# Expert items of 32 tokens in four column groups of TensorE, gate-up pieces of 256 whole rows

## The reference: what is computed

```python
logits = h @ w_router + b_router                 # 256 x 32
top_val, top_idx = lax.top_k(logits, 4)
weights = softmax(top_val)
for each expert e, for the tokens xb that chose it:
    gu = xb @ w_gate_up[e] + b_gate_up[e]        # 1024 -> 2048
    gate = minimum(gu[:, :1024], 7)
    up = clip(gu[:, 1024:], -7, 7)
    act = (up + 1) * gate * sigmoid(1.702 * gate)
    y = act @ w_down[e] + b_down[e]              # 1024 -> 1024
    out[token] += weight * y
```

```
42 53 27 40 37 42 25 48 33 27 25 21 24 29 35 26
32 23 25 33 37 35 29 26 34 24 19 22 33 43 27 48
```

## Time and profile before

| | us |
|---|---|
| median of 3 runs (1546.7 to 1549.62) | 1549.33 |
| the profiled execution's span | 1549.3 |
| TensorE busy | 97% |
| VectorE busy | 30% |
| ScalarE busy | 19% |

### The profile page before, as it was taken

The page is one execution under the profiler, slowest core; times in us unless marked ns, Lnnn a source line. Parts: engine busy times, 40 slices in busy tenths (PEclk is TensorE's granted clock), DMA queues, the critical chain, the costliest instruction groups (busy, mean ns, idle before and its releaser), DMA issues.

```text
span 1549.3 us, 21348 instructions
## 1 busy us (share of the span) xinstructions
PE 1502.3 (97%) x8793; PEld 775.7 (50%) x8794; DVE 472.4 (30%) x845; ACT 293.0 (19%) x457; POOL 36.9 (2%) x87
## 2 busy tenths in 40 slices
PE   6999899999999999999999999999999999999997
PEld 3875786633333333333333333333333686699643
DVE  2577442412121121211211112111111233466844
ACT  2224312211111111111111111111111233112100
POOL 6000210000000000000000000000000000000000
PEclk9999998999999999999999999999999999999999
DMA  9956104999999999999999999999999933244430
GB/s 373 314 213 243 56 3 195 405 397 429 426 429 428 428 429 429 428 429 429 429 428 429 429 428 430 428 428 429 428 427 428 363 109 109 109 164 164 175 151 27
DMA packets 71972, 503.32 MB, mean 325 GB/s; under 512 B 5278, under 2 KB 8496, under 8 KB 46320
## 3 DMA queue, kind: packets, MB, share of 16 engines
q1 hardware_dynamic: 71026, 500.25, 78.6%
q10 hardware_dynamic: 894, 2.30, 0.4%
HBM read 501.49 MB, written 1.05 MB: 324 GB/s over the span
## 4 chain that ended last, share of the span: by engine, by line
PE 81%; DMA 15%; DVE 2%; ACT 1%; issue 0%; SPq 0%; DVEq 0%
PE psum L1157 21%; DMA ring<-in_w_gate_up 13%; PE psum L1196 12%; PE psum L1458 6%; PE psum L1429 6%; PE psum L685 5%; PE psum L1114 3%; PE psum L1247 3%; PE psum L1098 3%; PE psum L614 3%; PE psum L1189 2%; PE psum L1032 2%; PE psum L1382 2%; DMA ring<-in_w_ada 2%; PE psum L1150 1%; PE psum L732 1%
## 5 line engine op out<-in xcount | busy, mean ns | idle before, releaser
L1157 PE MATMUL psum<-ring,work 128*64 128x512 f32 x2048 | 448.7, 594 | 11.3 <-DMA ring<-in_w_gate_up 11.3
L1157 PEld LDWEIGHTS psum<-ring,work 128*64 128x64 f32 x2048 | 142.6, 137 | 315.2 <-issue 289.2
L1196 PE MATMUL psum<-ring,work 128*64 128x512 f32 x1024 | 226.8, 595 | 0.0
L2235 DVE TENSOR_SCALAR work<-psum 128x512 f32<-128x512 f32 x32 | 22.1, 692 | 451.8 <-PE psum L1157 451.8
L1196 PEld LDWEIGHTS psum<-ring,work 128*64 128x64 f32 x1024 | 70.7, 137 | 153.9 <-issue 153.9
L1730 ACT ACTIVATE work<-work 128x512 f32<-128x512 f32 x32 | 20.1, 629 | 399.4 <-DVE work L2235 399.4
L685 PE MATMUL psum<-ring 128*128 128x256 f32 (+1 forms) x368 | 80.5, 380 | 0.4 <-ACT ring L1534 0.4
L685 PEld LDWEIGHTS psum<-ring 128*128 128x128 f32 (+1 forms) x368 | 68.5, 187 | 13.1 <-issue 2.1
L1114 PE MATMUL psum<-work 64*128 64x256 f32 x528 | 65.9, 389 | 0.7 <-ACT work L1736 0.7
L1736 ACT ACTIVATE work<-psum 128x512 f32<-128x512 f32 x32 | 19.1, 597 | 241.2 <-PE psum L1196 241.2
L1114 PEld LDWEIGHTS psum<-work 64*128 64x128 f32 x528 | 48.3, 186 | 31.9 <-issue 26.0
(11 more groups left out here) (476 smaller groups left out, 1533.9 us busy)
## 6 DMA issues: line engine op xcount, KB each, us to landing
ring<-in_w_gate_up SPq DMA_DIRECT2D x128, 2048.0 KB, 30.9
ring<-in_w_down SPq DMA_DIRECT2D x72, 2048.0 KB, 28.1
ring<-in_w_ada SPq DMA_DIRECT2D x12, 2048.0 KB, 12.4
ring<-in_w_up SPq DMA_DIRECT2D x8, 2048.0 KB, 7.8
ring<-in_w_in SPq DMA_DIRECT2D x6, 2048.0 KB, 7.9
ring<-in_w_out SPq DMA_DIRECT2D x4, 2048.0 KB, 7.9
ring<-in_w_in_sb SPq DMA_DIRECT2D x4, 2048.0 KB, 20.2
ring<-in_w_mem_kv SPq DMA_DIRECT2D x1, 2048.0 KB, 9.1
```

The costliest lines, as they stand in the source:

```text
L1157: ins = mm(B(1 + u)[CAP * h:CAP * (h + 1), :], xe[:, k % 4, k // 4, :], w[:, k % 2, c0:c0 + 512], start=False, stop=k == KT - 1)
L1196: last = mm(B(3)[CAP * h:CAP * (h + 1), :], act[:, k % 4, k // 4, :], w[:, k % 4, 512 * h:512 * (h + 1)], start=False, stop=k == KT - 1)
```

## The change

`CAP` becomes 32. An item is at most 32 tokens, so an expert with 33 to 64 tokens takes two passes, and `N_ITEM` grows from 48 to 64. With 32 columns in the stationary operand, four matmuls stand side by side, in four column groups (`GROUPS`). A group q computes 256 output columns (`GW`): in gate-up 256 of gate and 256 of up in one matmul of 512 columns, in down 256. The results of gate and up share one bank, 128 rows by 256 each.

```diff
-CAP = 64
+CAP = 32
+GROUPS = P // CAP
+GW = D // GROUPS
...
             def moe_src(e, j):
                 if j < 4:
-                    h, c0 = j // 2, 2 * (j % 2)
-                    return a["w_gate_up"][0, e, 512 * h:512 * (h + 1), :].rearrange(
-                        "(p c) n -> p c n", c=4)[:, c0:c0 + 2, :]
+                    return a["w_gate_up"][0, e, GW * j:GW * (j + 1), :].rearrange("(p c) n -> p c n", c=2)
...
             def freed(j, g):
                 if j < 4:
-                    sp_.wait_ge(S("e_gu"), g * 5 + [1, 2, 3, 5][j])
+                    sp_.wait_ge(S("e_gu"), g * 4 + (j + 1))
...
                 for ti in range(TT):
-                    for h in range(2):
-                        last = mm(B(0)[CAP * h:CAP * (h + 1), :], sel[:, ti, :],
-                                  tok[:, ti, 512 * h:512 * (h + 1)], start=ti == 0, stop=ti == TT - 1)
+                    for q in range(GROUPS):
+                        last = mm(B(0)[CAP * q:CAP * (q + 1), 0:GW], sel[:, ti, :],
+                                  tok[:, ti, GW * q:GW * (q + 1)], start=ti == 0, stop=ti == TT - 1)
...
             def scatter():
-                for c in range(4):
-                    for h in range(2):
-                        m = 4 * h + c
-                        last = mm(bank2(4 + m // 2)[:, m % 2, :], ye[CAP * h:CAP * (h + 1), c * P:(c + 1) * P],
-                                  selT[CAP * h:CAP * (h + 1), :], start=False, stop=False,
+                for j in range(2):
+                    for q in range(GROUPS):
+                        last = mm(bank2(4 + q)[:, j, :], ye[CAP * q:CAP * (q + 1), j * P:(j + 1) * P],
+                                  selT[CAP * q:CAP * (q + 1), :], start=False, stop=False,
                                   skip_group_check=True)
...
-                    for u in range(2):
-                        for h in range(2):
-                            r0 = E_N * (2 * u + h)
-                            mm(B(1 + u)[CAP * h:CAP * (h + 1), :], one_e[r0:r0 + E_N, :], bgu[r0:r0 + E_N, :],
-                               start=True, stop=False)
...
+                    for j in range(4):
+                        landed(j)
+                        w = ring[:, slots[j], :].rearrange("p (c u q n) -> p c q u n", c=2, u=2, q=GROUPS)
+                        for c in range(2):
+                            for q in range(GROUPS):
+                                last = mm(B(1)[CAP * q:CAP * (q + 1), :], xe[:, c, j, :], w[:, c, q, :, :],
+                                          start=j == 0 and c == 0, stop=j == 3 and c == 1)
                         last.then_inc(S("e_gu"), 1)
+                        if j == 0:
+                            for q in range(GROUPS):
+                                mm(B(1)[CAP * q:CAP * (q + 1), :], one_e[E_N * q:E_N * (q + 1), :],
+                                   bgu[E_N * q:E_N * (q + 1), :], start=False, stop=False)
...
                     for c in range(4):
-                        last = tr(B(3)[:, c * P:(c + 1) * P], act_tm[:, c * P:(c + 1) * P])
+                        for b in range(2):
+                            last = mm(B(2)[HD * b:HD * (b + 1), c * HD:(c + 1) * HD], act_tm[:, c * HD:(c + 1) * HD],
+                                      ident[:, :].rearrange("p (h b s) -> p b h s", h=2, b=2)[:, b, :, :],
+                                      start=True, stop=True)
```

More of the change, by code:

```diff
@@ L1146, in expert @@
                     pe.wait_ge(S("e_selT"), g + 1)
-                    for u in range(2):
-                        for h in range(2):
-                            r0 = E_N * (2 * u + h)
-                            mm(B(1 + u)[CAP * h:CAP * (h + 1), :], one_e[r0:r0 + E_N, :], bgu[r0:r0 + E_N, :],
-                               start=True, stop=False)
[L1153 to L1165, removed]
-                        last.then_inc(S("e_gu"), 1)
[L1167 to L1171, removed]
+                    for j in range(4):
+                        landed(j)
+                        w = ring[:, slots[j], :].rearrange("p (c u q n) -> p c q u n", c=2, u=2, q=GROUPS)
+                        for c in range(2):
+                            for q in range(GROUPS):
+                                last = mm(B(1)[CAP * q:CAP * (q + 1), :], xe[:, c, j, :], w[:, c, q, :, :],
+                                          start=j == 0 and c == 0, stop=j == 3 and c == 1)
+                        last.then_inc(S("e_gu"), 1)
+                        if j == 0:
+                            for q in range(GROUPS):
+                                mm(B(1)[CAP * q:CAP * (q + 1), :], one_e[E_N * q:E_N * (q + 1), :],
+                                   bgu[E_N * q:E_N * (q + 1), :], start=False, stop=False)
                     gather(g + 2)
@@ L1185, in expert @@
                     turn_x(g + 2)
+                    for q in range(GROUPS):
+                        mm(B(3)[CAP * q:CAP * (q + 1), 0:GW], one_e[E_N * q:E_N * (q + 1), :],
+                           b_down[E_N * q:E_N * (q + 1), :], start=True, stop=False)
                     pe.wait_ge(S("e_actT"), g + 1)
-                    for h in range(2):
-                        mm(B(3)[CAP * h:CAP * (h + 1), :], one_e[0:E_N, :], b_down[:, 512 * h:512 * (h + 1)],
-                           start=True, stop=False)
                     for k in range(KT):
@@ L1194, in expert @@
                         w = ring[:, slots[4 + k // 4], :].rearrange("p (k n) -> p k n", k=4)
-                        for h in range(2):
-                            last = mm(B(3)[CAP * h:CAP * (h + 1), :], act[:, k % 4, k // 4, :],
-                                      w[:, k % 4, 512 * h:512 * (h + 1)], start=False, stop=k == KT - 1)
+                        for q in range(GROUPS):
+                            last = mm(B(3)[CAP * q:CAP * (q + 1), 0:GW], act[:, k % 4, k // 4, :],
+                                      w[:, k % 4, GW * q:GW * (q + 1)], start=False, stop=k == KT - 1)
                         if k % 4 == 3:
@@ L1688, in _ @@
             ada_copy(9, 2)
-            dma(b_down, a["b_down"][0], S("bias_in"))
+            for q in range(GROUPS):
+                dma(b_down[E_N * q:E_N * (q + 1), :], a["b_down"][0, :, GW * q:GW * (q + 1)], S("bias_in"))
             for h in range(2):
@@ L2120, in _ @@
             V.tensor_reduce(wsh[:, :], w_sh.rearrange("p k e -> p e k"), AX.X, ALU.add).then_inc(*mark("wsh_ready"))
-            ch.add(V.memset(ye, 0.0))
+            ch.add(V.memset(nought, 0.0))
             ch.link(V.memset(selT, 0.0))
@@ L2200, in _ @@
             n_more = T // CAP - 1
-            for r in range(n_more):
-                ch.add(V.tensor_scalar(cnt[:, r, :], B(5)[0:1, 0:E_N], CAP * (r + 1) + 0.5, None, ALU.is_gt))
-            ch.wait()
-            for r in range(1, n_more):
-                ch.link(V.tensor_tensor(cnt[:, 0, :], cnt[:, 0, :], cnt[:, r, :], ALU.add))
-            ch.link(V.tensor_scalar(cnt[:, 0, :], cnt[:, 0, :], 1.0, None, ALU.add))
+            ch.link(V.tensor_scalar(cnt[:, n_more, :], B(5)[0:1, 0:E_N], -0.5, 1.0 / CAP, ALU.add, ALU.mult))
+            ch.link(V.tensor_tensor(cnt[:, 0:n_more, :], cnt[:, n_more:n_more + 1, :].broadcast_to([1, n_more, E_N]),
+                                    iota[0:1, 1:n_more + 1].unsqueeze(2).broadcast_to([1, n_more, E_N]), ALU.is_gt))
+            ch.link(V.tensor_reduce(cnt[:, n_more, :], cnt[:, 0:n_more, :].rearrange("p r e -> p e r"), AX.X, ALU.add))
+            ch.link(V.tensor_scalar(cnt[:, 0, :], cnt[:, n_more, :], 1.0, None, ALU.add))
             ch.add(V.tensor_copy(npass[:, :], cnt[:, 0, :]))
```

61 lines of the change are left out of this document (30 added, 31 removed).

## The result

| | before | after |
|---|---|---|
| median of the runs | 1548.27 us | 1589.01 us |
| runs | 4, 1546.7 to 1549.62 | 4, 1584.82 to 1589.36 |
| ratio, 95% interval | | 1.0253 [1.0234, 1.0271] |
| the execution profiled: time, span | 1549.3, 1549.3 | 1584.82, 1583.1 |

The change costs 40.7 us, 2.5%. The forecast was slower by 30.7, at 1580 with 1566 to 1604. The execution profiled after the change is the fastest of the four, 4.2 us under their median, so its stages sum to less than the median does.

What follows compares the result with a forecast made beforehand. Transfers were taken to set the end, so cheaper items only wait longer. Start 16.4 us, second gap 2.8 and the extra pass at the end gave +30.2, plus 0.5 for the clock: 1580 us, own range 1575 to 1590, wider 1566 to 1604.

Steps and rivals of the forecast that it cites:

- The bound: In the experts, TensorE and transfers are nearly equal limits; transfers at 428 GB/s, 29.37 us an expert, set the end.
- The number of items and the price of one: TensorE's expert work: 47 items instead of 32, each 16.1 us against 27.9; a two-pass expert 32.2 us.
- The start: Expert 0's first pass must finish before any slot is free, so the first slot comes 16.4 us later.
- a second gap: Transfers pause again at two-pass expert 1, waiting for the next slot: 2.8 us.
- The end: After the last piece, expert 31 needs half a down (1.8 us) and a whole item (16.1 us).
- the walk through the experts: All 32 experts followed one by one with these prices: no third gap, last piece at 1224.9 us.
- dearer items: Rival: form changes or short matmuls make items cost more, 1587 us at 17.1 us each; about 1605, chance 0.08.
- The clock: TensorE's clock drops when idle in one-pass experts, hidden by waiting; 0.5 us added at expert 31.
- groups not side by side: Rival: TensorE's four groups reach 0.8 of fourfold, item 19 us, time 1630 us; chance 0.04.
- The delay made good: Rival: transfers were not full before, so the start's delay is recovered and only the end counts, about 1561 us; chance 0.07.
- Faster transfers by whole rows: Rival: contiguous 2 MB gate-up pieces move faster; 443 GB/s instead of 428 would pay back 30.2 us; chance 0.03.
- more dips follow after expert 1: Sign in the changed profile that the prediction is wrong; it expected two GB/s dips, slices 9 and 10, then 428.

Runs made afterwards that it cites:

- turn by 12: The changed kernel with experts taken in the order 12 to 31, 0 to 11, so one-pass experts stand at both ends: 1554.45 us, ratio 1.0044.
- turn by 15: The changed kernel with experts in the order 15 to 31, 0 to 14, first two one-pass, last two-pass: 1567.66 us, ratio 1.0135.
- the kernel written out: The changed kernel in its own order with 30 experts written out instead of a loop over 5: 1587.16 us, ratio 1.0246.
- the loop of three: The changed kernel in its own order of experts, with nine slots in use and a loop over 3 experts: 1582.35 us, ratio 1.0215.
- The nine-slot kernel turned by 12 and written out: The changed kernel in the order 12 to 31, 0 to 11, nine slots in use, 30 experts written out: 1557.49 us, ratio 1.0043.
- The loop of three with nine slots: The changed kernel in the order 12 to 31, 0 to 11, nine slots in use, loop over 3 experts: 1548.41 us, ratio 0.9998.
- the turn by 19: The changed kernel with experts in the order 19 to 31, 0 to 18, first two two-pass, last one-pass: 1577.65 us, ratio 1.0188.
- before, written out: The kernel before with 30 experts written out instead of 6 rounds over 5: 1555.07 us, ratio 1.003.

## Why the prediction was right, and what it missed

**The bound.** Right: TensorE's 114 us of saved work bought nothing, since the transfers set the end. In the turn by 12 all of the change but the two ends is within 0.5% of before.

**The number of items and the price of one.** 47 as forecast. The item is 15.6 us instead of 16.1. The term off is the scatter: I kept 1.9 between the bounds 1.0 and 1.9, and it takes 1.15 to 1.25. Four row groups do give most of the gain that I excluded by the pair rate of the earlier trace rows. A two-pass expert is 31.1.

**The start.** Forecast: first slot 16.4 us later, a second gap of 2.8. Measured: 22.0 - 4.86 = 17.2 later, of which the wait for the item lists is 3.01 (forecast 3.1), and a second gap of 31.06 less 29.4, 1.7. Together 18.9 against 19.2. The runs give more, 23.2 for a start with experts 19, 20, 21 (three of two passes instead of two) and 21.3 from the turn by 15 to the change, because they compare with a changed kernel whose first slot is free after 2.1 us, 2.7 earlier than that of the kernel before.

**The end.** Forecast 17.9 us behind the last piece, measured 1247.35 - 1229.95 = 17.4. Before, the last piece was followed by 1212.56 - 1205.7 = 6.9 us (its landing being the estimate of the prediction), so the extra pass costs 10.5 us at the end where the forecast had 11. The runs' 13.2 and 11.4 compare with a last expert of one pass, as said there.

**The step that failed.** In the paragraph on the slots I wrote that no third gap arises and that the pace stays 428 GB/s, so that the last piece is used 919.2 us after the start. It was 929.0. Piece 65 is used at 605.63 and piece 191 at 1229.95: 126 pieces in 624.3 us, 4.955 each instead of 4.895, so 7.5 us lie there and the rest before. The dip to 392 in the 24th slice is some 3.2 us of it (35 of 427 over a slice of 39.6 us). It follows the jump at 897.06 with its wait of 6.43, ahead of experts 20 and 21 with two passes each, and in this order of experts it is in neither the kernel written out nor the loop of three. The nine-slot kernel turned by 12 and written out, which has no stalls, does show a smaller dip, 414 in its 27th slice; so the stall alone is not shown to be the cause. The rest goes with the fetches. The loop of three checks the forecast without them: its last piece is used 1231.50 - 307.53 = 924.0 us after the start, and with nine slots one piece more, 4.9 us, has to come behind the first free slot. With ten slots that would be 919.1 (an estimate), and the forecast was 919.2. So the walk through the experts was right, and the 9.8 us come from what it left out. I had counted what each edit does to the instructions' time, and not to their number: an item of the earlier trace rows is 142 matmuls with 142 loads, one of now 196 with 196, so a body of five experts grew from 1420 to 1960 of them, waits and branches not counted, while three experts of now are 1176.

**The sum.** The ratios step up as 1.0044 (ends of one pass), 1.0135 (last expert of two), 1.0253 (the change): 7, 14 and 18 us; the medians give 5.4, 13.2 and 21.3. The first step is itself a sum, here as an estimate from the traces. The turn by 12 uses its last piece after 908.7 us. The loop of three with nine slots does after 902.2, which less 4.9 for the piece more is 897.3: fetches and jumps cost 11.4. The earlier first slot gives 2.8 back (2.1 us after the start instead of 4.86), the shorter work behind the last piece 5.0 (1.9 instead of 6.9), and the longer stretch behind the experts takes 2.5 (339.2 instead of 336.7). That is 6.1 us, within the 5 to 7 measured.

**How much of it was luck.** The measured 1589 is 9 us above the forecast and only just inside my own range, which ended at 1590. The room above 1580 was reckoned with dearer items (1587 at 17.1 us each); the item took 15.6, and the room was used up by something that I had not thought of. The sign, the two ends and the limit by transfers were right by mechanism; that the total stayed in the range of 1575 to 1590 was partly luck.

**The clock.** As forecast: it fell where TensorE waits, the waits hid it. After the jumps 16 matmuls took 3.4 to 3.64 us instead of 1.92; from 451.80 to 455.30 the granted clock was 0.54, near the lower level, and from 455.30 on 1.00. I gave it 0.5 us at expert 31; there 1219.94 shows 3.44 us for piece 3, but TensorE still waited 0.83 us for the last piece of down, so it cost nothing.

**The rivals.** Dearer items and groups not side by side: no, by the item above. The delay made good: no, the turn by 19 keeps it to the end. Faster transfers by whole rows: no, 1.0002. Of my signs one fired, "more dips follow after expert 1", and it pointed at the one thing that the forecast lacked.

What stays open: why 36 fetches of 16 KB in 700 us cost some 5 us of transfers in that stretch (2.07 MB less of weights) and 9 us in all. Their bytes explain 1.4. No run tells whether they take one DMA engine's turn, or how. How the 9.8 us of the change divide between the fetches and the stalls at the jumps stays open too: the kernel written out has no stalls and takes the same time within the spread of its runs.

## What to carry to other kernels

Where transfers set the end, ask of a faster compute step only two things: when does the first buffer come free, and how much work stands behind the last transfer. Here 15 second passes cost 32 to 35 us at three places and nothing at the others. And count the instructions of a loop's body, not only their time: a body of 1960 put code on the DMA engines in every round where one of 1420 did not. A loop of three was 9.1 us faster than the same items written out, and 6.7 us faster than the change even with one slot less.

## What the hardware showed unexpectedly

A loop's code stays in TensorE up to some size. Bodies of 1176 and of 1420 matmuls and loads were not fetched again between 450 and 1150 us; one of 1960 was, in every round. The counts of fetches agree with blocks of 256 instructions: some 24 experts run from 450 to 1150 us, 24 x 392 / 256 = 37, and the change written out shows 37 (before, written out: 24 x 284 / 256 = 27, shown 28). The change in its loop shows 47, ten more for five jumps, as if what was fetched ahead past the jump were thrown away; that is argued, not shown. The Trainium skill (Runtime: NRT & Kernel Launch, "Instruction fetch mechanics") gives TensorE 2048 instructions of its own memory in blocks of 256, and the trace agrees with both, if waits and branches bring 1960 above 2048. It also says, with no exception for TensorE, that only two such blocks are held and that a jump beyond them stalls; the kernel before jumps over 1420 without a fetch or a stall, so for TensorE the measurement says otherwise. The stall itself it has right for the body of 1960: 6.3 to 6.7 us at each of the five jumps.

Four column groups of TensorE side by side gave the full four: 64 matmuls of 512 moving columns in 7.0 us, 109 ns each, where two groups gave 215.5. Four row groups with 128 stationary columns took 1.15 us for 16 instructions where two took 2.0.
